# Second attention: each head's exponentials in two parts, turned tiles by chunk and head

## The reference, cut to what matters

```python
_, sel = lax.top_k(s_idx, k_top)                  # 256 keys of each query, by an index score
lg_s = einsum('bqhc,bqkc->bqhk', ql, c_sel) * scale + bias      # -inf where not causal
lg_m = ...                                        # the same for 16 meta tokens
p = softmax(concatenate([lg_m, lg_s], axis=-1), axis=-1)
out = einsum('bqhm,bmc->bqhc', p[..., :N_META], c_m) + einsum('bqhk,bqkc->bqhc', p[..., N_META:], c_sel)
```

## Time and profile before

| | |
|---|---|
| Time, median of 3 runs | 3507.48 us (3506.69 to 3513.3) |
| The profiled execution: time, span | 3508.17 us, 3506.2 us |
| Mean granted TensorE clock, as a share of full speed | 0.972 |
| Attention of group 0, 1, 2, 3, about | 1788 to 1855, 2191 to 2298, 2650 to 2815, 3203 to 3432 us |
| TensorE busy | 3315.4 us, 95% |
| ScalarE busy | 1399.5 us, 40% |
| All exponentials of the second attention | 128 instructions |

### The profile page before, as it was taken

How to read it: one execution, slowest core, us unless ns; L and a number is a source line. 1 busy time by engine, 2 the same in 40 slices (tenths; PEclk the granted TensorE clock), 3 DMA queues, 4 the chain that set the end, 5 groups by cost and what they waited for, 6 DMA issues and landing times.

```text
span 3506.2 us, 49804 instructions
## 1 busy us (share of the span) xinstructions
PE 3315.4 (95%) x18464; PEld 2043.4 (58%) x18464; DVE 2001.2 (57%) x4950; ACT 1399.5 (40%) x2644; POOL 707.3 (20%) x1093
## 2 busy tenths in 40 slices
PE   9999999999999999999989999999998898998887
PEld 3444577567656755745557455674556673555566
DVE  3417733763475357435563577835768636878743
ACT  2312312322231313133241475515875515886542
POOL 0016032112101210111131101211451121352011
PEclk9999999999999999989989999999999999998999
DMA  5226135204401420341204210041210051110004
GB/s 193 78 77 244 34 121 174 102 19 128 155 2 52 148 78 2 94 159 54 64 25 153 73 60 28 25 150 54 68 44 1 25 159 48 58 52 1 1 1 132
DMA packets 114161, 275.23 MB, mean 78 GB/s; under 512 B 11097, under 2 KB 12673, under 8 KB 111873
## 3 DMA queue, kind: packets, MB, share of 16 engines
q1 hardware_dynamic: 105584, 256.31, 22.5%
q10 hardware_dynamic: 8336, 15.74, 1.3%
HBM read 239.75 MB, written 32.26 MB: 78 GB/s over the span
## 4 chain that ended last, share of the span: by engine, by line
PE 80%; DVE 8%; ACT 6%; issue 5%; POOL 1%; DMA 0%; ACTq 0%; DVEq 0%; POOLq 0%; SPq 0%
PE bank L2325 25%; PE bank L2339 17%; PE o_acc L2497 6%; PE bank L2480 6%; PE bank L2727 3%; PE bank L2614 3%; PE bank L2487 3%; PE bank L2646 3%; PE bank L2739 2%; PE o_acc L2753 2%; PE bank L2576 1%; ACT prob_t L1474 1%; ACT index L1615 1%; PE bank L2398 1%; PE bank L2404 1%
## 5 line engine op out<-in xcount | busy, mean ns | idle before, releaser
L2325 PE MATMUL bank<-group_even,weights 128*128 128x512 f32 x1152 | 508.2, 598 | 9.4 <-DMA group_even<-in_x_t 5.7
L2325 PE MATMUL bank<-group_odd,weights 128*128 128x512 f32 x960 | 425.3, 598 | 2.8 <-ACT tmp L1460 2.8
L2325 PEld LDWEIGHTS bank<-group_even,weights 128*128 128x128 f32 x1152 | 218.7, 192 | 275.2 <-issue 275.0
L1419 ACT ACTIVATE probs<-probs,stat 128x512 f32<-128x512 f32 x256 | 181.7, 711 | 432.1 <-DVE stat L1743 432.1
L2325 PEld LDWEIGHTS bank<-group_odd,weights 128*128 128x128 f32 x960 | 181.6, 192 | 222.4 <-issue 221.9
L2497 PEld LDWEIGHTS o_acc<-lat,val 128*128 128x128 f32 x2048 | 240.6, 196 | 49.9 <-issue 41.3
L2497 PE MATMUL o_acc<-lat,val 128*128 128x128 f32 x2048 | 250.1, 282 | 13.3 <-DVE lat L1863 13.3
L2480 PE MATMUL bank<-k_nope,q_nope 128*32 128x512 f32 x2048 | 233.0, 595 | 0.0
L1849 DVE CUSTOM_DVE_ANT_0 probs<-bank,mask 128x512 f32<-128x512 f32 x256 | 161.4, 686 | 95.7 <-PE bank L2487 95.7
L2727 PE MATMUL bank<-kh,qa 64*128 64x512 f32 (+3 forms) x816 | 176.7, 516 | 13.9 <-DVE o_sb L2285 7.5
L1863 DVE STREAM_TRANSPOSE lat<-probs 128x512 f32<-128x512 f32 x256 | 168.8, 695 | 20.3 <-ACT probs L1419 19.0
(11 more groups left out here) (463 smaller groups left out, 6124.3 us busy)
## 6 DMA issues: line engine op xcount, KB each, us to landing
weights<-in_w_in SPq DMA_DIRECT2D x101, 512.0 KB, 3.6
weights<-w_sums SPq DMA_DIRECT2D x200, 256.0 KB, 3.4
weights<-in_w_out SPq DMA_DIRECT2D x96, 256.0 KB, 3.6
weights<-in_w_in_q SPq DMA_DIRECT2D x28, 512.0 KB, 3.5
weights<-in_w_in_q SPq DMA_DIRECT2D x54, 256.0 KB, 3.4
w_sums<-group_odd SPq DMA_DIRECT2D x10, 1024.0 KB, 4.7
weights<-in_w_i SPq DMA_DIRECT2D x20, 512.0 KB, 3.7
group_odd<-in_x_t SPq DMA_DIRECT2D x8, 1024.0 KB, 8.4
```

Source lines behind the costliest of these rows:

```text
L1419: A_(p, p, ACT.Exp, scale=QK_DIM ** -0.5, bias=stat[:, 16 + PARTS * (n % 2) + r:17 + PARTS * (n % 2) + r], accum_out=sums_1[:, i % 2, PART ...
L2325: ins = M(bank(*name)[:], ring[n % SLOTS][:, k * P:(k + 1) * P], rhs[:, k, :], start=(k == 0), stop=(k == chunks - 1))
```

## The change

Three things change for the second attention, and nothing else.

First, the exponential of a head is done in two instructions where n is over 512: the columns 0 to 511, then the rest. The order is: head 0 first part, head 1 first part, head 0 rest, head 1 rest. Each part has its own place for its row sum, and each signals `probs2_made`. With n up to 512 (group 0) there is one part, as before.

Second, the first turned tiles of a unit come in the order chunk 0 of head 0, chunk 0 of head 1, chunk 1 of head 0, chunk 1 of head 1, in place of both chunks of head 0 and then both of head 1. TensorE waits for the first part ahead of chunk 0, and for the second part ahead of chunk 1.

Third, VectorE adds the row sums of both parts, so one more small addition for each block with n over 512.

```diff
+def exp_parts(i):
+    n = keys_of(i)
+    return [(0, min(TB, n))] + ([(TB, n)] if n > TB else [])
+
+def exps_before(i, p):
+    return 2 * (PAIRS * sum(len(exp_parts(b)) for b in range(i)) + p * len(exp_parts(i)))
...
-        yield from [("turn", u, e, c) for e in range(2) for c in range(min(2, count))]
+        yield from [("turn", u, e, c) for c in range(min(2, count)) for e in range(2)]
...
-        sums2 = alloc(two, "sums2", [P, 2, H2])
+        sums2 = alloc(two, "sums2", [P, 2, 2, H2])
...
-                        for e in range(2):
-                            n = H2 * i + 2 * p + e
-                            act.wait_ge(row_max2, n + 1)
-                            scores = probs_of(g, u, e)
-                            A_(scores, scores, ACT.Exp, bias=stat[:, 8 + n % 8:9 + n % 8],
-                               accum_out=sums2[:, i % 2, 2 * p + e:2 * p + e + 1]).then_inc(probs2_made, 1)
+                        for part, (first, end) in enumerate(exp_parts(i)):
+                            for e in range(2):
+                                n = H2 * i + 2 * p + e
+                                act.wait_ge(row_max2, n + 1)
+                                scores = probs_of(g, u, e)[:, first:end]
+                                A_(scores, scores, ACT.Exp, bias=stat[:, 8 + n % 8:9 + n % 8],
+                                   accum_out=sums2[:, i % 2, part, 2 * p + e:2 * p + e + 1]).then_inc(probs2_made, 1)
...
-                        dve.wait_ge(probs2_made, H2 * (i + 1))
-                        step(dve, V.tensor_tensor(stat[:, 24:32], stat[:, 24:32], sums2[:, i % 2, :], ALU.add))
+                        dve.wait_ge(probs2_made, exps_before(i + 1, 0))
+                        for part in range(len(exp_parts(i))):
+                            step(dve, V.tensor_tensor(stat[:, 24:32], stat[:, 24:32], sums2[:, i % 2, part, :], ALU.add))
...
-                        if c == 0:
-                            pe.wait_ge(probs2_made, H2 * i + h + 1)
+                        if c < len(exp_parts(i)):
+                            pe.wait_ge(probs2_made, exps_before(i, p) + 2 * c + e + 1)
```

## The result

The changed kernel takes 3523.39 us (median of 17 runs, 3512.4 to 3529.82); the kernel before, measured beside it, 3506.89 us (17 runs, 3502.28 to 3514.43). The ratio is 1.0039, with an interval of 1.0031 to 1.0047: slower by 0.39%, 11 to 16 us. The profiled execution took 3515.71 us, span 3513.6, against 3508.17 and 3506.2 before. Of all timed runs one, of the kernel "cut at 1024, copies late", took 9561 us at a mean clock of 0.605; it counts in no ratio and no mean here.

A forecast was written before the change was run, and what follows sets the result against it. TensorE, busy 95% of the span, was taken as the bound, with about 43 us of waits for exponentials in groups 2 and 3. Terms 2.3 + 2.3 + 0.4 = +5.0 us on 3507.48 gave 3512.5 us, range 3503 to 3521.

The forecast's parts named there:

- The likeliest case: Whole kernel: measured time within about 0.2%, 7 us, of the kernel before; chance 0.60.
- Exponentials in two parts: ScalarE, second attention: each second part costs a fixed 0.29 us a head, so a pair's last part ends 0.58 us later.
- The order of turning, and the end of the unit: Groups 2 and 3: four tiles, not eight, follow the last exponential; unit ends +0.14 us later, +2.3 us in sum.
- The rival of the first wait: Turning in groups 2 and 3: the shorter first wait is what counts, 29 us less, 3478 us; chance 0.05.
- The copies behind the exponentials: Copies of turned tiles start 0.58 us later; four TensorE waits in group 1 lengthen, +2.3 us; hidden in groups 2 and 3.
- just hidden: Group 1, nearest case without a wait for a copy: 0.7 us to spare against the 0.58 us delay, so no cost.
- The rival "in all of group 1": Later copies hold TensorE in 14 units of group 1, 8.1 us in place of 2.3, giving 3518.3 us; chance 0.10.
- The small things: VectorE's second addition of row sums in 12 blocks, two of them counted: +0.4 us, bounds 0 and 2.4.
- The sum without the clock: Whole kernel: unit ends 2.3, copies 2.3 and small things 0.4 add up to +5.0 us.
- The clock: Group 3, rival of more half clock: two more slow windows, +5.6 us on top of +5.0, 3518.1 us; chance 0.15.
- the two windows named there: Group 3: two windows of 8 us with granted clock 0.69 and 0.62, 11.2 us at half clock, 5.6 us lost.
- The sign that I had named for it: Group 3: granted clock leaving 0.94 by more than 0.02, 5 us on 235 us of TensorE's work, would show the forecast wrong.

The follow-up runs named there:

- cut at 1024, copies late: Against the kernel before, groups 2 and 3 only: exponentials cut at column 1024, old turning order, the rest done at once ahead of the copies; 3512.05 us, ratio 1.0005.
- The order alone: Against the kernel before: one exponential for each head as before, only the order of the turned tiles changed; 3532.80 us, ratio 1.0073.
- the cut at 1024: Against the kernel before, groups 2 and 3 only: exponentials cut at column 1024, old turning order, the rest behind the copies of chunks 0 and 1; 3486.30 us, ratio 0.9926.
- group 1 alone: The change applied in group 1 only, other groups as in the kernel before; 3513.19 us, ratio 1.0015 to the kernel before.
- the parts alone: Against the kernel before: exponentials in two parts, turned tiles in the old order; 3516.52 us, ratio 1.0028.

## Why the prediction was right and wrong

**The likeliest case didn't come.** I gave 0.60 to no difference beyond 0.2% and 0.30 to slower; it is slower by 0.39%. 3512.5 us was forecast, 3523.39 measured, beyond the range's upper end of 3521 as a median, and at it by the ratio (1.0039 x 3507.48 = 3521.2). The direction of the sum was right, its size a third of what came. Most of what is missing is the clock, which had 0 in the sum.

**Exponentials in two parts**: right. 0.29 us for each added part was forecast, 0.28 measured for an extra one, and the pair's last part ended 0.55 us later (4.54 against 3.99), not 0.58.

**The order of turning, and the end of the unit**: right. +0.14 us a unit was forecast, +0.12 measured from pair to scores, +0.13 from pair to pair (14.59 against 14.46). The waits ahead of the last two turnings are 0.73 and 0.90 us, not 1.1: turning began 0.84 us sooner, not the 1.28 that was reckoned from the exponential alone, and four tiles by themselves hold TensorE for 0.66 us. The order alone gives +0.44, the parts with the old order +0.12, the cut at 1024 -1.70: the end of the unit moves with the last part for which chunks 0 and 1 wait, and with the tiles behind it. The rival of the first wait is out. Groups 2 and 3: +2.3 forecast, +2.5 at full clock; at 0.37 for a microsecond of half clock it would be +3.7.

**The copies behind the exponentials**: the size nearly right, the term a little too small, its working only in part. +2.3 us was forecast for group 1; from pair to pair +2.6 was found in the profile, +3.5 to +4.5 at full clock in the timed runs. Three units with a wait for copies grew by the 0.58 us forecast and one without by 0.44, but TensorE's waits for copies rose from 2.6 to 4.0 us in the changed kernel (4.7 in group 1 alone), not to 5. The rest, 0.1 to 0.2 us in some units that I had put down as just hidden, is small. The rival "in all of group 1" is out: it would have given 8.1. In groups 2 and 3 the copies cost nothing in the change, as said; the cut at 1024 with late copies shows from where on they do, and that I under-counted there, one wait where several follow one another.

**The small things**: the second addition of row sums can't be seen apart; 0.4 us stands unproved.

**The sum without the clock**: +5.0 forecast, +6 to +7 measured (3413.6 and 3414.0 at full clock against 3406 to 3408), +8 at 0.37 for each microsecond at half clock. The later part of the profiles gives +5.1 to +6.9 in three of five.

**The clock**: the step that failed. It was a rival with 0.15 and +5.6 us, and 0 in the sum, because the idle time stays the same (the two windows named there give 11.0 us at half clock, not 11.2). In the profiled executions TensorE's idle time even fell a little, from 191 us (3506.2 - 3315.4) to 186 (3513.6 - 3328.1). But the half-clock time rose: over the timed runs by 13 us (25 runs of the change, 49 of before), which costs 5 us at the 0.37 found from run to run and 6 to 7 at one half. That is between a third and a half of the whole loss, and more than any term that I had worked out. The sign that I had named for it, the clock of group 3 leaving 0.94 by more than 0.02, didn't show: it was 0.93. Whether more idle is needed for more half clock: the parts alone have the same units and 12 us less of it; the order alone, with 0.44 us more idle in a unit, has 32 us more, and there the profile shows it fall in the changed units.

What isn't shown is where the timed runs of the change have theirs. Its five profiles have 138 to 172 us in the later part, 150 on average, and before has 149 and 150. Of the two profiled executions over 3520 us, one lost its time ahead of the second attention, in instructions that the change doesn't touch, the other behind, 3.1 us of it in one unit. So that the change brings the half clock is shown by the timed runs alone; by which idle piece, and why, stays open.

## What to carry to other kernels

When a wait is cut into pieces, ask which piece ends last and what stands behind it; bringing the first piece forward is worth nothing if the last moves back. Cut where the consumer's first need ends (here 1024 columns, not 512), and put the rest where nobody waits for it: the same two instructions gave +14 us in one place and -26 in the other. And look at what is queued behind the pieces on their own engine: with the copies behind the rest, nearly the whole gain was gone.

## What the runs showed of the hardware

The number of waits and their sum in the profile fell (18.4 to 14.4 us in group 2) while the unit got longer; the starts from unit to unit repeated to 0.01 us at equal clock and showed it. Stage lengths repeated to 0.02 us in some executions of the same kernel (group 1 took 102.27 us in three profiles) and then took another value (101.84, 101.69). At equal instructions, executions of the change differ by 11 us in the later part, with 34 us more at half clock. From run to run of one kernel a microsecond at half clock went with 0.34 to 0.44 us of span, not with half of one (the kernel before and the change, 74 runs). And changes whose units differ by a few tenths of a microsecond (order alone against before) moved the half-clock time by 32 us: on this kernel, a term of under 5 us can't be told from the clock by one profile.
